# Bidirectional retention inside a two-layer trunk: two heads worked side by side on operands left in place, values centred when they are projected, one root and one reciprocal for the variances of four heads

## The reference

```python
mu = jnp.mean(o, axis=-1, keepdims=True)
var = jnp.mean(jnp.square(o - mu), axis=-1, keepdims=True)
o = (o - mu) * lax.rsqrt(var + EPS)
o = o.reshape(o.shape[0], o.shape[1], -1) * lp['ret_gn_g'].astype(jnp.float32)
return (o.astype(g.dtype) * jax.nn.silu(g)) @ lp['w_br_ret']
```

## Time and profile before

| | |
|---|---|
| median of 3 runs | 6162.94 us (6155.7 to 6170.76) |
| profiled execution, first to last instruction | 6142.2 us |
| its distance to the median | 20.7 us |
| PE / DVE / ACT busy share of the span | 82% / 70% / 30% |
| mean granted TensorE clock | 0.895 of full |
| retention stage C, layer 0 | 86.1 us |
| retention stage X, layer 0 | 164.9 us |
| retention stage X, layer 1 | 164.1 us |

### The profile page before, as it was taken

How to read it: one execution, slowest core, us unless ns; L and a number is a source line. 1 busy time by engine, 2 the same in 40 slices (tenths; PEclk the granted TensorE clock), 3 DMA queues, 4 the chain that set the end, 5 groups by cost and what they waited for, 6 DMA issues and landing times. The chain is left out here.

```text
span 6142.2 us, 70319 instructions
## 1 busy us (share of the span) xinstructions
PE 5047.4 (82%) x23958; PEld 4032.6 (66%) x23958; DVE 4290.9 (70%) x7337; ACT 1872.9 (30%) x3261; POOL 859.6 (14%) x644
## 2 busy tenths in 40 slices
PE   7687727979566777999999878988794669999998
PEld 5385726723455566898888747723673559999997
DVE  1547577768885687999999842368635977677676
ACT  1222312222122264333333311221122653333333
POOL 0000005500342000333333200000000001111110
PEclk8797868989788888999999979979897789999999
DMA  6142317711574256999999911201121357777775
GB/s 215 72 148 72 106 39 294 283 34 55 177 259 154 93 166 201 388 398 397 393 395 394 357 59 67 97 8 62 59 86 35 83 155 272 275 276 273 274 275 196
DMA packets 465582, 1172.61 MB, mean 191 GB/s; under 512 B 225331, under 2 KB 259540, under 8 KB 412438
## 3 DMA queue, kind: packets, MB, share of 16 engines
q1 hardware_dynamic: 373272, 633.88, 30.2%
q0 software_dynamic: 92160, 536.91, 22.8%
HBM read 1106.46 MB, written 64.23 MB: 191 GB/s over the span
## 5 line engine op out<-in xcount | busy, mean ns | idle before, releaser
L2178 POOL DMA_INDIRECT arena<-in_peer_uv,kept x384 | 519.0, 1352 | 3657.9 <-POOLq L2063 2016.0
L223 PE MATMUL psum<-h_hi,u_ring_hi 128*128 128x384 f32 x2048 | 694.1, 339 | 18.4 <-DVE ring_lo L2266 18.1
L223 PE MATMUL psum<-h_hi,ring_lo 128*128 128x384 f32 x2048 | 694.8, 339 | 0.0
L223 PE MATMUL psum<-h_lo,u_ring_hi 128*128 128x384 f32 x2048 | 694.1, 339 | 0.0
L223 PE MATMUL psum<-v_ring_hi,w_hi 128*128 128x512 f32 x1536 | 609.4, 397 | 6.4 <-DVE ring_lo L2271 6.4
L223 PE MATMUL psum<-ring_lo,w_hi 128*128 128x512 f32 x1536 | 603.5, 393 | 0.0
L223 PE MATMUL psum<-v_ring_hi,w_lo 128*128 128x512 f32 x1536 | 600.4, 391 | 0.0
L2271 DVE TENSOR_TENSOR ring_lo<-kept,v_ring_hi 128x1024 fp32r<-128x1024 f32 x256 | 313.8, 1226 | 300.2 <-ACT v_ring_hi L2226 295.1
L2310 DVE SCALAR_TENSOR_TENSOR arena<-arena 128x1024 f32<-128x1024 f32 x384 | 482.0, 1282 | 19.2
L2298 DVE CUSTOM_DVE_ANT_0 arena<-arena 128x1024 f32<-128x1024 f32 x384 | 462.5, 1219 | 31.0 <-DMA arena<-in_peer_uv,kept 29.9
L2238 ACT ACTIVATE w_hi<-arena 128x384 fp32r<-128x384 f32 x256 | 134.7, 526 | 964.9 <-DVE arena L2281 964.9
(11 more groups left out here) (348 smaller groups left out, 10245.7 us busy)
## 6 DMA issues: line engine op xcount, KB each, us to landing
kept<-in_mix SPq DMA_DIRECT2D x312, 512.0 KB
kept<-in_peer_u SPq DMA_DIRECT2D x256, 512.0 KB
kept<-in_peer_uv SPq DMA_DIRECT2D x256, 512.0 KB
kept<-in_ada SPq DMA_DIRECT2D x96, 512.0 KB
gate_scratch<-arena SPq DMA_DIRECT2D x12, 4096.0 KB, 20.8
arena<-gate_scratch SPq DMA_DIRECT2D x128, 384.0 KB
spec_scratch<-arena SPq DMA_DIRECT2D x4, 2048.0 KB, 8.5
arena<-in_k_dft_x SPq DMA_DIRECT2D x6, 1024.0 KB, 9.9
```

The source lines that it names most:

```text
L223: done = pe.matmul(out, lhs[x], rhs[y], start=first and j == 0, stop=last and j == 2)
L2178: pool.indirect_dma_start(rows[q % NBUF], None, peer_uv, bass.IndirectOffsetOnAxis(ap=row_id[q % G][:, q // G:q // G + 1], axis=0))\
```

## The change

- `keep_v` no longer copies. It sums each token's 128 values of the head (`tensor_reduce` from PSUM), drains, and writes v minus a 128th of that sum. The head's output then has mean zero over channels, so the mean matmul, the copy from PSUM, and the subtraction are gone.
- The retention stage is unrolled over four pairs of heads. q, k, v and the context's k and v are read where they lie; the staging copies and the `staged` wait are gone. For each key tile there are two score matmuls in a row, head 0 of the pair on partitions 0 to 63 and head 1 on 64 to 127, into different PSUM banks, and then two value matmuls into banks 4 and 5.
- The first product of the exponents moves from VectorE (L1086) to ScalarE (`backward`, a Copy with a scale, into the table itself).
- ScalarE squares each head's output straight from PSUM, and VectorE gates it from PSUM (`gate`: output times gain times gate) before it is normalized. The first value matmuls of the next pair wait for both squares and both gates.
- `variance` multiplies the squares with a matrix that has one column of 1/128, at column 32 x row, so that four heads' variances gather in rows 0, 32, 64 and 96 of one bank. One root and one reciprocal serve four heads. `spread` brings a row back to 128 partitions with a matmul one row deep, and `normalize` multiplies it into the gated output. For X, the first four heads are spread and normalized inside the last pair; for C, and for the last four heads of both, this stands at the end.

```diff
                     def keep_v(i, k):
                         dve.wait_ge(blocks_done.sem, blocks_done.at(4 * i + (n_qk + k + 1)))
-                        dve.tensor_copy(v[:, :, ds(4 * P * i + k * P, P)],
-                                        ps[:, k, 0:T].rearrange("p (a b) -> p a b", b=P)).then_inc(bank_free.sem, 1)
+                        x = ps[:, k, 0:T].rearrange("p (a b) -> p a b", b=P)
+                        dve.tensor_reduce(head_sum[:, k % 2], x, AX.X, ALU.add)
+                        dve.drain()
+                        dve.scalar_tensor_tensor(v[:, :, ds(4 * P * i + k * P, P)], head_sum[:, k % 2].unsqueeze(2).broadcast_to([P, nt, P]),
+                                                 -1.0 / DV, x, ALU.mult, ALU.add).then_inc(bank_free.sem, 1)
...
+                    def backward(c, h):
+
+                        head = 2 * c + h
+                        if c >= 2:
+                            act.wait_ge(prob_ready.sem, prob_ready.at(2 * NJ * (c - 1)))
+                        act.activation(tables[c % 2][h], lag, ACT.Copy, scale=back_rate[:, head:head + 1])\
+                           .then_inc(back_ready.sem, 1)
...
+                    def square(c, h):
+                        act.wait_ge(value_done.sem, value_done.at(2 * NJ * c + 2 * NJ))
+                        if h == 1:
+                            act.wait_ge(gated.sem, gated.at(2 * c + 1))
                         if c > 0:
+                            act.wait_ge(var_ready.sem, var_ready.at(2 * c))
+                        act.activation(sq[h], ps[:, OUT[h], 0:T], ACT.Square).then_inc(squared.sem, 1)
...
+                    def score(i):
+
+                        c, j = divmod(i, NJ)
+                        kind, jt = tiles[j]
+                        if i >= 2:
+                            pe.wait_ge(prob_ready.sem, prob_ready.at(2 * i - 2))
+                        for h in range(2):
+                            rows = slice(DK * h, DK * h + DK)
+                            if kind == "own":
+                                k = qk[rows, (4 + c) * T + jt * P:(4 + c) * T + jt * P + P]
+                            else:
+                                k = ctx_k[rows, c, jt * P:jt * P + P]
+                            pe.matmul(ps[:, SCORE[2 * (i % 2) + h], 0:T], k, qk[rows, c * T:c * T + T], start=True, stop=True)\
+                              .then_inc(score_ready.sem, 1)
+
+                    def values(i):
+
+                        c, j = divmod(i, NJ)
+                        kind, jt = tiles[j]
+                        x = v if kind == "own" else ctx_v
+                        if j == 0 and c > 0:
+                            pe.wait_ge(squared.sem, squared.at(2 * c))
+                            pe.wait_ge(gated.sem, gated.at(2 * c))
+                        for h in range(2):
+                            head = 2 * c + h
+                            pe.wait_ge(prob_ready.sem, prob_ready.at(2 * i + h + 1))
+                            pe.matmul(ps[:, OUT[h], 0:T], x[:, jt, head * P:head * P + P], prob[i % 2][h],
+                                      start=j == 0, stop=j == NJ - 1).then_inc(value_done.sem, 1)
...
+                    def spread(n, row):
+
+                        pe.wait_ge(rs_ready.sem, rs_ready.at(n + 1))
+                        if n == 0 and row > 0:
+                            pe.wait_ge(normed.sem, normed.at(row))
+                        if n == 1 and row != 1:
+                            pe.wait_ge(normed.sem, normed.at(max(4, 2 + row + 1)))
+                        bank = VAR if n == 1 and row % 2 else SPREAD
+                        pe.matmul(ps[:, bank, 0:T], ones[32 * row:32 * row + 1, :], rs[32 * row:32 * row + 1, :],
+                                  start=True, stop=True).then_inc(spread_ready.sem, 1)
+
+                    score(0)
+                    score(1)
+                    for i in range(PAIRS * NJ):
+                        c, j = divmod(i, NJ)
+                        if i + 2 < PAIRS * NJ:
+                            score(i + 2)
+                        values(i)
+                        if c > 0 and j == 1:
+                            variance(c - 1)
+                        if c == 3:
+                            for row in SPREADS.get(j, ()):
+                                spread(0, row)
+                    variance(PAIRS - 1)
+                    for row in range(4):
+                        spread(1, row)
...
                     for i in range(PAIRS * NJ):
                         c, j = divmod(i, NJ)
                         probabilities(i)
                         if c > 0 and j == 0:
                             gate(c - 1)
```

More of the change, by code:

```diff
@@ L1013, in _ @@
+                    for h in range(2):
+                        square(PAIRS - 1, h)
+                    root(1)
                 @block.tensor
                 def _(pe):
[L1015 to L1021 removed]
@@ new lines, in variance @@
+                    def variance(c):
+                        if c == 2:
+                            pe.wait_ge(root_ready.sem, root_ready.at(1))
+                        for h in range(2):
+                            row = 2 * (c % 2) + h
+                            pe.wait_ge(squared.sem, squared.at(2 * c + h + 1))
+                            pe.matmul(ps[:, VAR, 0:T], pick_row[:, 96 - 32 * row:224 - 32 * row], sq[h],
+                                      start=row == 0, stop=row == 3).then_inc(var_ready.sem, 1)
@@ L1127, in stage_retention @@
+                    gate(PAIRS - 1)
+                    dve.drain()
+                    for row in late_norms:
+                        normalize(0, row)
+                    invert(1)
+                    for row in range(4):
+                        normalize(1, row)
             consts_in.add(32)
-            for c in (act_a, act_b, root_ready, pe_b, dve_b, mean_ready, var_ready, squared, exponents, staged):
+            dve_a.add(1)
+            for c in (back_ready, exponents, act_a, squared, gated, var_ready, spread_ready, normed):
```

269 lines of the change are left out of this document (123 added, 146 removed).

## The result

The changed kernel takes 6023.85 us (median of 4 runs, 6013.99 to 6026.45) against 6162.33 us for the kernel before (4 runs, 6155.7 to 6170.76): ratio 0.9775, 95% interval 0.9763 to 0.9788, 138.5 us less. In the X stage of layer 0 the changed kernel writes one of its tables, the backward exponents for the context, over 104 of each token's 128 weights of the context's gathered experts, which a later stage still needs; a part of the computation is changed by it. `e17` moves the table and takes 6026.38 us, so the gain does not come from that.

A forecast was written before the change was run, and what follows sets the result against it. TensorE was taken to bound the X stages, losing time to form changes, pair copies and the clock. 6142.2 - 78 (X) - 28 (C) + 4.4 (projections) = 6040.6, with 20.7 on top 6061 us; 8-in-10 range 6035 to 6092.

The forecast's parts named there:

- 4.4 more for the projections: Projections: reduction, drain and two-operand pass per v block add 2.4 us in three projections, 2 in layer 0's X projection.
- The 20.7 us: Whole kernel: difference between profiled span and median of the runs, added to the 6040.6 us span to give 6061.
- the middle value: X-stage body: two scores cost three records' time for four, 1.28 us, making a step 3.37 us; chance 0.42.
- fully beside: Rival: two heads' scores overlap wholly, a step falls to 2.95 us, kernel 6040 us; chance 0.17.
- a sign that it was wrong: Listed signs: clock at 0.50 past the first pair, step of 3.8 or 2.95 us, or TensorE waiting for probabilities.
- The body's allowances: X-stage body: 5 us for the clock and 3 for boundaries, reciprocal and such, within a body of 96 us.
- Start and tail: X stage: first values after 15.7 us; tail from last value 13.5 us, where it was 12.1.
- The C stage: C stage: first values after 11.6 us, then 31, tail 15; sum 58, so 28 us less.
- VectorE's chain: C stage: VectorE's chain of a pair, about 7 us, stays below TensorE's 9.
- Reading in place: X stage: TensorE waited 24.3 us for pair copies, 18.0 at the start, about 2.1 at each of three later pairs.
- clock stays down: Rival: the two-by-two order never raises the clock, an X stage takes 210 us, kernel 6231 us; chance 0.04.
- Its counter-argument: Against the clock rival: the clock rose in a run of 128-row matmuls, as every step now has one.

The follow-up runs named there:

- e17: Changed kernel with squares and the context's backward exponents swapped in the layout, so no needed weights are written over; 6026.38 us, ratio 0.9783.
- e7: The alternating order of e3 with twelve unneeded 128-row matmuls behind the first scores of each retention stage; 6078.35 us, ratio 0.9876 to the kernel before.
- e2: Changed kernel with both scores of a pair read from partitions 0 to 63; 6065.31 us, ratio 0.9843 to the kernel before.
- e10: Changed kernel with the last four heads' spreads sent at once into four score banks, in C also the first four's; 6008.85 us, ratio 0.9752.
- e1: The changed kernel run again as base of the first group; 6019.88 us, ratio 0.9759 to the kernel before.
- e5: Kernel before, heads unrolled, with q, k, v and context read in place and no pair copies; 6104.33 us, ratio 0.9906.
- e4: Changed kernel with a plain copy of v instead of the centring, without reduction and drain; 6023.67 us, ratio 0.9759 to the kernel before.
- e9: The changed kernel run again as base of the third group; 6023.34 us, ratio 0.977 to the kernel before.
- e3: Changed kernel with score and values of head 0, then of head 1, in alternating order on TensorE; 6142.34 us, ratio 0.9964 to the kernel before.
- e12: Kernel before with the hardware loop over heads 2 to 5 written out; 6157.01 us, ratio 0.9991, X stages 158.9 and 167.9 us.

## Why the prediction was too high

**The sum.** Forecast were 39 us less for each X stage and 28 for C, 4.4 more for the projections: 102 less. Measured: 55.1, 52.8 and 32.4 in the stages. The stages account for 34 of the 37 us between 6061 and the median, and the 4.4 of the projections, which did not come, for the rest. The 20.7 us by which the sum was lifted from the span to the median were no cost at launch: the changed kernel's profiled execution has a span of 6022.5 and a time of its own of 6025.1 us, 2.6 apart. With as much on top, an estimate, that of the kernel before took some 6145 us: a short one among runs that scatter from 6147.65 to 6181.92 us over all groups.

**What two scores cost: the step that failed.** I took the middle value, three records' time for four, because "the second record of head 0 can lie beside the first of head 1 and nothing else can". The four records lie in 1.13 us, and one such matmul after a form change takes 1.12 (`e7`): head 1 costs 0.01 us. The timeline of 3963.30 to 3963.75 shows which lie together:

```profile
3963.26 0.70 PE L1048 MATMUL psum<-arena 64*128 64x512 f32 x2
```

Two records fit in 0.70 us, and one alone takes 0.69, so a record of head 0 and one of head 1 run beside each other from the start, and the other two after them; nothing had to wait for head 0's second record. The rival with "fully beside", at a chance of 0.17, named the time of a step, 2.95; measured 2.97, which the prediction had listed as a sign that it was wrong. The Trainium skill, TensorE: Matmul & The Clock Gate, section Part 3: Packing small matmuls — row/col tiling, gives a packed group the duration of one matmul and about 4 ns for each further tile. The trace agrees, with 0.01 us for the second, and it is so for f32, whose matmul has two records. `e2` shows that this is the halves' doing: 22 steps at 0.86. Against the middle value it is 0.40 a step, 9 us an X stage and some 3 in C. That alone would have given about 6040, so it is 21 of the 37 us; the rest is sizes, below.

**The body's allowances.** From the first values to the last, the last X stage took 79.8 us (3959.92 to 4039.68) where I had 96. 9 are the scores. The clock cost the first values 1.4 us (3.41 against 1.98) where I added 5; the three boundaries cost 1.6 us of waiting in all, where I added 3 for them and the like. The other 2 to 3 us are two items counted in the body that lie outside it: the first pair of scores stands ahead of the first values (3957.91), and the fourth spread behind the last values (4039.57); each of these is little over 1 us. With the measured prices (21 steps with scores at 2.97, three without at 1.91, six variances 5.2, three spreads 3.2, boundaries with their hand-overs 1.8, clock 1.4) the sum is 79.7. All these allowances pointed one way: each was an upper guess added to a sum that was meant to be the likeliest.

**Start and tail.** 15.8 us to the first scores of the body, 17.8 to the first values, where I had 15.7: two cold scores stand between. Tail 13.7 against 13.5. Both right to 2 us, the tail in part by luck: its terms as listed add up to 15 to 16 us, not to 13.5. Its four spreads were overestimated, while what their taking turns with VectorE costs was not seen; `e10` shows it.

**The C stage.** First values after 12.6 us (11.6 forecast), tail from 471.3 to 486.7, 15.3 (15). Between them 25.7 us instead of 31: scores beside each other, and a clock that rises, mean 0.63 where I had it at 0.50 throughout, as in the earlier trace rows. Four score records take 1.23 us at its start, 0.70 from 450.67 on, and 1.22 again at 461.14, after a wait; in `e1` the clock did not fall there. The prediction held that VectorE's chain stays below TensorE's in C. With scores beside each other and the clock up it doesn't: TensorE waits 1.64 us for probabilities at 454.60 and again at 461.14:

```profile
461.14 1.22 PE L1048 MATMUL psum<-arena 64*128 64x256 f32 x4 [1.64 <-DVE arena L1132]
```

**Reading in place.** The copies' waits were rightly read as lost time. `e5` alone gains 57.8 us, where 40 to 45 were worked out from these waits, because less waiting also kept the clock up. Added to the 45 us that `e2` gives to the halves it makes 103 of the 138.5; fewer form changes are about 7 us an X stage (`e7` against `e1`, less the 19 of the halves). The rest, with the variances and reciprocals by fours, was not tried apart; the two need not add up, since the clock is in both.

**Centring.** 4.4 us were put on it; `e4` and `e1` have the same ratio, and the matmuls that make v are spread no further apart in `e9` than before. Its rows in the changed kernel are as long as forecast, 0.69 us each for the sum and for the subtraction in an X projection, and TensorE's work on the next block covers them.

**The clock.** The rival "clock stays down" (0.04) did not come true for the order of the change, and `e3` shows that it was real: the same matmuls in alternation stay at 1.2 GHz for 66 us. Its counter-argument held: the clock rose where 128-row matmuls stand in a row, after two with values in the change, after three in all stages of `e3`. Between `e3` and `e1` lie 122 us, but not all is the clock's, since the alternation also takes the scores of a pair apart: of 56 to 57 us an X stage 31 are the clock (`e3` against `e7`), 19 the halves and some 7 the form changes.

## What to carry to other kernels

Put matmuls that use half the rows in a row with their other half: the second cost 0.01 us here, in f32, and four spreads one row deep took no longer than two. Order matmuls of different depth in runs, not in alternation, and look at the granted clock before you cost a stage; copies on which TensorE waits cost their time and mostly the clock after it (five of six waits in the kernel before). What then remains is at a stage's ends: fetch its tables a stage early and let short matmuls of a tail go out together.

Whoever takes the changed kernel over should take the layout of `e17` with it: in the X stage of layer 0 the second table of L952, the changed kernel's backward exponents for the context, ends 104 columns inside `ctx_weight`, which still holds weights for the context's gathered experts.

## What was not expected of the hardware

TensorE, busy without a gap for 66 us with 64-row and 128-row f32 matmuls in turn, stayed at a granted clock of 0.50 (`e3`), while the two-by-two order reached 1.00 within 6 us of its first scores, and once twelve 128-row matmuls had raised it, it stayed at 1.00 through the same alternation (`e7`, X stages). In `e3` it rose in all three stages in the first run of three 128-row matmuls. Such a run is not always enough: with 256 columns, in the C stage of `e7`, two of them (462.87 and 473.85) left it at 0.50. What it is about the alternation that keeps the clock down is open, and so is why a wait of 2.0 us brought it down in one of the two like stages of `e12` and not in the other.
